# A hybrid attention step on one core: the gates computed in the combined projection instead of between the tiles of the prompt's attention

## The chip, the core and the metric

The kernel runs on one core of one Trainium2 chip. The metric is the device time of one execution in microseconds (us). A core has a matrix engine (TensorE, PE in the profile; PEld is its weight load), VectorE (DVE), ScalarE (ACT), GpSimd (POOL), and SyncE (SP), whose queue here only starts DMAs. Each runs its own instructions in order; semaphores tie them together.

## The reference, cut to what matters

Two layers, each over nine tiles of 128 rows: eight of the prompt (1024 rows) and one of the running streams (8 streams of 16 rows).

```python
h = jnp.einsum('bsd,de->bse', x, w_in)          # 1024 -> 7592 columns
(a_q, a_k, a_v, a_f, a_g, b_q, b_k, b_v, b_g,
 c_ql, c_kvl, c_pe, c_g, gates) = jnp.split(h, IN_OFFSETS, axis=-1)
...                                              # three attentions, 8 heads each
up = jnp.einsum('bsnw,nwd->bsnd', br, w_br)
mixed = (jax.nn.sigmoid(gates.reshape(B, S, 3, D_MODEL)) * up).sum(axis=2)
y = jnp.einsum('bsd,de->bse', mixed, w_o)
```

`gates` are the last 3 x 1024 columns of the combined projection. They are needed only in the up projection, after all attention. Attention a is causal over 1024 keys with forgetting, b sees at most 256 keys and has a sink, c is block-causal over 1024 keys.

## The kernel before

Phases run one after the other, with a barrier between them: per layer the projection, two small phases (forget sums, latent keys), the prompt's attention a, b and c, the streams' attention, the up projection and the output projection. Intermediate results go through scratch tensors in HBM.

**Precision.** A product of fp32 quality is made of three fp32r matmuls: weights and activations are each split into a high and a low part, and high x high, high x low and low x high are summed (L351 to L353, L1056 to L1058). The activations' parts, `xh` and `xl`, stay in SBUF from the projection to the end of attention c.

**Projection** (`projections`, tile names `proj_`). `CHUNKS` lists nine column chunks, all but one 512 wide (the last 424). Each chunk goes over the nine row tiles: 8 x 3 matmuls into one of eight PSUM banks, then ACT or DVE turns the bank into `out`, and SP stores it. While chunk c is multiplied, ACT (L321) and DVE (L326) split the weights of chunk c+1, and SP loads those of c+2. So TensorE has its weights ready one chunk ahead.

**Prompt attention** (`prompt_attention`, names `att_a_`, `att_b_`, `att_c_`). Four passes, each over a pair of heads; a pass has 16 steps, n = 0 to 15, of 128 queries each (the first 8 are one head, the rest the other; a = n mod 8 is the query tile). In a and c a step works on a+1 key tiles, in b on at most 2. The order of each engine's work is one list, `order`, and for each step it has

- `turn` n: TensorE transposes the probabilities (L1027); DVE, and ACT for the first four tiles where there are more than four, copy them to SBUF as `pt` (L1128, L1085);
- `score` n+2: TensorE makes the logits two steps ahead (L1009, mask L1012, in b a sink column L1005); DVE takes the maximum (L1133), ACT the exponential (L1091);
- `fill`, in nine steps of sixteen: one row tile of a gate strip 256 columns wide (below);
- `prep`, in eight steps: a transposition of queries or keys for a later head (L995);
- `pv` n: probabilities times values (L1045), which needs `pt`; then DVE scales and stores to `o` (L1172).

```python
fills = [0, 1, 2, 6, 7, 8, 9, 14, 15]
...
for n in range(K):
    order += [("turn", n), ("score", n + 2)]
    if n in fills:
        order.append(("fill", fills.index(n)))
    if n in preps:
        order.append(("prep", preps[n]))
    order.append(("pv", n))
```

The last pass has no `prep` for a further head and no `score` in steps 14 and 15. A fill is 24 matmuls of 256 columns into one PSUM bank `gacc`, followed by a tanh on ACT into `gout` (L1105; the up projection makes the sigmoid of it). A pass covers one strip for all nine row tiles; four passes make the 1024 gate columns of a branch. A strip's weights come in one DMA (L910) and are split into `gwh` and `gwl`: for the first pass by ACT (L1118) and DVE (L1185), for the others by GpSimd (L968, L970) during the pass before. `gout` is stored in three parts (L916).

SP's queue of a pass: queries and keys of the next pass, gate weights, a gate store, then the store of the first head's output (L902), a wait for its landing, the load of that head's next values (L897) and of its output gates `sg` (L898), two gate stores, and the same for the second head.

Of the kernel before, what the change touches and what calls it, by code (L numbers as in the profile page):

```python
# [21 lines left out]
F32 = mybir.dt.float32  # L22
F32R = mybir.dt.float32r
# [191 lines left out]
def norm_rows(nc, dve, ch, x, gb, st, mv, var_ready, std_ready, t, normed):  # L215
# [16 lines left out]
    ("silu_c", [(O_CG, 512)]),  # L232
    ("cq_bk", [(O_CQ, QR), (O_BK, 128)]),
# [6 lines left out]
def projections(nc, C, T, S, l):  # L240
# [45 lines left out]
    with nc.Block() as block:  # L286
# [95 lines left out]
        def _(act):  # L382
# [20 lines left out]
            for c in range(NCH):  # L403
                kind, u = CHUNKS[c][0], c % 2
                for t in range(NT):
# [9 lines left out]
                    elif kind.startswith("silu"):  # L415
                        nc.scalar.activation(sig[:, j, :], bank, ACT.Sigmoid).then_inc(sig_ready, 1)
                    elif kind in ("cq_bk", "bv_ckv"):
# [101 lines left out]
def _scratch(name):  # L519
    return lambda T, S, l, t: S[name][t * P:(t + 1) * P]  # L520


_HEADS = ("l b s h d -> l (b s) (h d)", "l b s h d -> l (b s) (h d)")
# [8 lines left out]
    "silu_c": [(0, 512, _scratch("sg2"))],  # L532
    "cq_bk": [(0, QR, _scratch("ql")), (QR, 512, _scratch("kb"))],
# [230 lines left out]
def prompt_attention(nc, C, T, S, l, kind):  # L764
# [27 lines left out]
    xh, xl = C["xh"], C["xl"]  # L792
    GW = D // (H // 2)
    graw = ph.sb("graw", [P, KT, GW])
    gwh = ph.sb("gwh", [P, 2 * KT, GW], F32R)
    gwl = ph.sb("gwl", [P, 2 * KT, GW], F32R)
    gout = ph.sb("gout", [P, NT, GW])
    gacc = ph.ps("gacc", [P, 512])
    gw_loaded, gw_hi, gw_lo = ph.sem("gw_loaded"), ph.sem("gw_hi"), ph.sem("gw_lo")
    g_made, g_taken, g_stored = ph.sem("g_made"), ph.sem("g_taken"), ph.ring("g_stored", 3)  # L800
# [25 lines left out]
    fills = [0, 1, 2, 6, 7, 8, 9, 14, 15]  # L826
    preps = {2: (1, 0), 3: (1, 1), 4: (1, 2), 5: (1, 3), 10: (2, 0), 11: (2, 1), 12: (2, 2), 13: (2, 3)}
    assert len(fills) == NT
    order = []
    for n in range(K):  # L830
        order += [("turn", n), ("score", n + 2)]
        if n in fills:
            order.append(("fill", fills.index(n)))
        if n in preps:
            order.append(("prep", preps[n]))
        order.append(("pv", n))
# [41 lines left out]
    with nc.Block() as block:  # L878
        @block.sync
        def _(sp):  # L880
# [25 lines left out]
            wsrc = T["w_in"].rearrange("l (k p) n -> l p k n", p=P)  # L906

            def load_gate(pair):
                col = O_GATE + D * branch + GW * pair
                sp.dma_start(graw[:], wsrc[l, :, :, ds(col, GW)]).then_inc(gw_loaded, 16)  # L910

            def store_gate(pair, part):

                ts = slice(part * NT // 3, (part + 1) * NT // 3)
                sp.wait_ge(g_taken, 1 + NT * pair + ts.stop)
                sp.dma_start(S["gates"].rearrange("(t p) c -> p t c", p=P)  # L916
                             [:, ts, ds(D * branch + GW * pair, GW)], gout[:, ts, :]).then_inc(g_stored[part], 16)


            sp.sem_inc(g_taken, 1)  # L920
            for part in range(3):
                sp.sem_inc(g_stored[part], 16)
            load_qk(0, 0)
            load_gate(0)
# [3 lines left out]
            with sp.Fori(0, H // 2 - 1) as i:  # L928
                sp.wait_ge(tr_made, group(i, 0))
                load_qk(i + 1, 0)  # L930
                sp.wait_ge(gw_lo, i + 1)
                load_gate(i + 1)
                store_gate(i, 0)
# [5 lines left out]
                store_gate(i, 1)  # L939
                store_gate(i, 2)  # L940
# [3 lines left out]
            store_gate(H // 2 - 1, 0)  # L944
            store(H // 2 - 1, 0)
            store_gate(H // 2 - 1, 1)
            store_gate(H // 2 - 1, 2)
# [3 lines left out]
            for part in range(3):  # L951
                sp.wait_ge(g_stored[part], 16 * (H // 2 + 1))

        @block.gpsimd
        def _(pool):

# [7 lines left out]

            def split(pair, at):

                pool.wait_ge(gw_loaded, 16 * (pair + 1))
                nc.gpsimd.tensor_copy(gwh[:, ds(at, KT), :], graw[:]).then_inc(gw_hi, 1)  # L968
                pool.wait_ge(gw_hi, pair + 1)
                nc.gpsimd.tensor_tensor(gwl[:, ds(at, KT), :], graw[:], gwh[:, ds(at, KT), :].bitcast(F32),  # L970
                                        ALU.subtract).then_inc(gw_lo, 1)


            pool.wait_ge(gw_hi, 1)
            split(1, KT)
            with pool.Fori(0, H // 2 - 2) as i:
                pool.wait_ge(g_made, NT * (i + 1))
                split(i + 2, KT * (i & 1))

        @block.tensor  # L980
        def _(pe):
# [33 lines left out]
            def body(i, order, at):  # L1015
                for what, n in order:
# [31 lines left out]
                    elif what == "fill":  # L1048
                        if n == 0:
                            pe.wait_ge(gw_lo, i + 1)  # L1050
                        pe.wait_ge(g_taken, 1 + NT * i + n)
                        first = KT * (i & 1)
                        for kt_ in range(KT):
                            hi, lo = (m[:, kt_, n * P:(n + 1) * P] for m in (xh, xl))
                            wh, wl = (m[:, ds(first + kt_, 1), :].rearrange("p k n -> p (k n)") for m in (gwh, gwl))
                            nc.tensor.matmul(gacc[:, 0:GW], hi, wh, start=kt_ == 0, stop=False)  # L1056
                            nc.tensor.matmul(gacc[:, 0:GW], hi, wl, start=False, stop=False)  # L1057
                            mm = nc.tensor.matmul(gacc[:, 0:GW], lo, wh, start=False, stop=kt_ == KT - 1)  # L1058
                        mm.then_inc(g_made, 1)
# [23 lines left out]
        def _(act):  # L1083
# [10 lines left out]
            def body(i, order, at):  # L1094
                for what, n in order:
# [5 lines left out]
                    if what == "fill":  # L1101
                        if n % 3 == 0:
                            act.wait_ge(g_stored[n // 3], 16 * (i + 1))
# [1015 lines left out]
```

## Time and profile before

| | us |
|---|---|
| median of three runs | 3794.53 |
| their range | 3792.19 to 3799.66 |
| the profiled execution, its own time | 3789.74 |
| its span, first to last instruction | 3788.1 |
| TensorE busy | 3390.3 |
| DVE / ACT / GpSimd busy | 1411.7 / 885.1 / 125.5 |
| mean granted clock of TensorE | 0.952 of 2.4 GHz |

The profile is one execution. Times of rows count from the span's start. A matmul's duration in a row runs to its modelled end and overlaps with the next one, so what a stream of matmuls costs is read from start to start, not from the durations. The two layers run the same program; the first layer's stretches are shown.

### The profile page before, as it was taken

What the parts mean: (1) busy time and instruction counts of PE and PEld (TensorE: products, weight loads), DVE (VectorE), ACT (ScalarE), POOL (GpSimd) and SP (SyncE); (2) the same over time, 40 slices, a digit from 0 to 9 for tenths busy, and PEclk for the clock granted to TensorE, in tenths of its full rate; (3) what the DMA queues carried; (4) which work ended last, traced back from release to release, by engine and by line L of the source; (5) the groups of instructions that cost most, each with busy time, mean ns of one, the idle gap of its engine ahead of it and who ended that gap; (6) DMA issues with size and microseconds to landing.
All of it is one profiled execution on the core that took longest, in us unless ns stands there. A gap on an engine that the chain in (4) does not pass through costs nothing. (4 is left out here: it accounts for less than half of the span.)

```text
span 3788.1 us, 54850 instructions
## 1 busy us (share of the span) xinstructions
PE 3390.3 (89%) x20866; PEld 2834.0 (75%) x20866; DVE 1411.7 (37%) x3261; ACT 885.1 (23%) x1982; POOL 125.5 (3%) x64
## 2 busy tenths in 40 slices
PE   0999978998998997989969999789989999978988
PEld 0888865887997885667758888568879878855877
DVE  5114233333343332354631233334333333323556
ACT  1221212332222332220221112123322233322110
POOL 0000000100100000000000000000000001000000
PEclk9999988999999998989979999889999989988999
DMA  5322225221433225753442222342233243186533
GB/s 194 106 89 94 77 89 160 62 64 39 108 76 98 59 72 142 244 220 126 144 153 92 88 91 67 120 123 64 64 74 91 60 98 87 37 231 212 218 129 107
DMA packets 485460, 423.06 MB, mean 112 GB/s; under 512 B 300452, under 2 KB 394532, under 8 KB 482916
## 3 DMA queue, kind: packets, MB, share of 16 engines
q1 hardware_dynamic: 451444, 381.06, 33.7%
q10 hardware_dynamic: 33840, 39.66, 3.2%
q8 instruction: 110, 1.80, 0.2%
q14 instruction: 66, 0.54, 0.0%
HBM read 295.36 MB, written 127.64 MB: 112 GB/s over the span
## 5 line engine op out<-in xcount | busy, mean ns | idle before, releaser
L351 PE MATMUL proj_acc<-proj_wh,keep_xh 128*128 128x512 f32 (+1 forms) x1296 | 502.1, 387 | 12.5 <-DVE proj_wl L326 12.5
L352 PE MATMUL proj_acc<-proj_wl,keep_xh 128*128 128x512 f32 (+1 forms) x1296 | 500.8, 386 | 0.0
L353 PE MATMUL proj_acc<-proj_wh,keep_xl 128*128 128x512 f32 (+1 forms) x1296 | 500.7, 386 | 0.0
L351 PEld LDWEIGHTS proj_acc<-proj_wh,keep_xh 128*128 128x128 f32 x1296 | 244.5, 189 | 58.4 <-DVE proj_wl L326 13.3
L352 PEld LDWEIGHTS proj_acc<-proj_wl,keep_xh 128*128 128x128 f32 x1296 | 244.6, 189 | 45.7
L353 PEld LDWEIGHTS proj_acc<-proj_wh,keep_xl 128*128 128x128 f32 x1296 | 244.4, 189 | 45.7
L1820 PE MATMUL up_acc<-up_wh,up_bh 128*128 128x512 f32 x432 | 173.1, 401 | 12.8 <-DVE up_wl L1864 12.8
L326 DVE TENSOR_TENSOR proj_wl<-proj_raw,proj_wh 128x512 fp32r<-128x512 f32 (+1 forms) x144 | 96.1, 676 | 210.6 <-ACT proj_wh L321 210.6
L1056 PE MATMUL att_c_gacc<-att_c_gwh,keep_xh 128*128 (+1 forms) x576 | 170.7, 296 | 2.9 <-DVE att_c_gwl L1185 2.9
L1056 PE MATMUL att_b_gacc<-att_b_gwh,keep_xh 128*128 (+1 forms) x576 | 170.7, 296 | 2.3 <-DVE att_b_gwl L1185 2.3
L1056 PE MATMUL att_a_gacc<-att_a_gwh,keep_xh 128*128 (+1 forms) x576 | 169.9, 295 | 1.9 <-DVE att_a_gwl L1185 1.9
L1821 PE MATMUL up_acc<-up_wl,up_bh 128*128 128x512 f32 x432 | 170.4, 394 | 0.0
L1822 PE MATMUL up_acc<-up_wh,up_bl 128*128 128x512 f32 x432 | 170.2, 394 | 0.0
L1057 PE MATMUL att_c_gacc<-att_c_gwl,keep_xh 128*128 (+1 forms) x576 | 164.7, 286 | 0.0
L1057 PE MATMUL att_b_gacc<-att_b_gwl,keep_xh 128*128 (+1 forms) x576 | 164.6, 286 | 0.0
L1058 PE MATMUL att_c_gacc<-att_c_gwh,keep_xl 128*128 (+1 forms) x576 | 164.6, 286 | 0.0
L1058 PE MATMUL att_b_gacc<-att_b_gwh,keep_xl 128*128 (+1 forms) x576 | 164.5, 286 | 0.0
L1057 PE MATMUL att_a_gacc<-att_a_gwl,keep_xh 128*128 (+1 forms) x576 | 163.9, 285 | 0.0
L1058 PE MATMUL att_a_gacc<-att_a_gwh,keep_xl 128*128 (+1 forms) x576 | 163.6, 284 | 0.0
L1091 ACT ACTIVATE att_a_p<-att_a_ss,att_a_stat 128x128 f32<-128x128 f32 (+7 forms) x128 | 95.1, 743 | 255.5 <-DVE att_a_stat L1133 255.4
L1091 ACT ACTIVATE att_c_p<-att_c_ss,att_c_stat 128x128 f32<-128x128 f32 (+7 forms) x128 | 95.1, 743 | 252.9 <-DVE att_c_stat L1133 252.9
L1009 PE MATMUL att_a_ss<-att_a_kt,att_a_qt 66*128 66x512 f32 (+3 forms) x384 | 148.3, 495 | 1.7 <-DVE att_a_kt L1128 1.7
(338 smaller groups left out, 6803.6 us busy)
## 6 DMA issues: line engine op xcount, KB each, us to landing
up_gates<-scratch_gates SPq DMA_DIRECT2D x18, 1536.0 KB, 8.3
proj_raw<-in_w_in SPq DMA_DIRECT2D x48, 512.0 KB, 3.8
str_ka<-in_cache_a_kT SPq DMA_DIRECT2D x16, 1024.0 KB, 9.0
str_va<-in_cache_a_v SPq DMA_DIRECT2D x16, 1024.0 KB, 5.3
scratch_sg<-proj_out SPq DMA_DIRECT2D x54, 256.0 KB, 2.1
up_br<-scratch_br SPq DMA_DIRECT2D x54, 256.0 KB, 8.2
scratch_gates<-att_a_gout SPq DMA_DIRECT2D x24, 384.0 KB, 2.6
scratch_gates<-att_b_gout SPq DMA_DIRECT2D x24, 384.0 KB, 2.7
```

The costliest lines, as they stand in the source:

```text
L326: nc.vector.tensor_tensor(wl[:, u, kt, 0:w], raw[:, kt // 2, kt % 2, 0:w], wh[:, u, kt, 0:w].bitcast(F32), ALU.subtract).then_inc(w_ready[ ...
L351: nc.tensor.matmul(bank, hi, wh[:, u, kt, 0:w], start=kt == 0, stop=False)
L352: nc.tensor.matmul(bank, hi, wl[:, u, kt, 0:w], start=False, stop=False)
L353: mm = nc.tensor.matmul(bank, lo, wh[:, u, kt, 0:w], start=False, stop=kt == KT - 1)
L1009: nc.tensor.matmul(ss[:, s, c:c + cw], lhs, kt[:, u, first + c:first + c + cw], start=True, stop=not last)
L1056: nc.tensor.matmul(gacc[:, 0:GW], hi, wh, start=kt_ == 0, stop=False)
L1057: nc.tensor.matmul(gacc[:, 0:GW], hi, wl, start=False, stop=False)
L1058: mm = nc.tensor.matmul(gacc[:, 0:GW], lo, wh, start=False, stop=kt_ == KT - 1)
L1091: nc.scalar.activation(p[:, s, 0:w], ss[:, s, 0:w], ACT.Exp, bias=stat[:, s, 0:1], accum_out=stat[:, s, 1:2]).then_inc(exp_ready, 1)
L1820: nc.tensor.matmul(acc[:, a, :], bh[:, u, k, :], wh[:, k, cols], start=k == 4 * n, stop=False)
L1821: nc.tensor.matmul(acc[:, a, :], bh[:, u, k, :], wl[:, k, cols], start=False, stop=False)
L1822: mm = nc.tensor.matmul(acc[:, a, :], bl[:, u, k, :], wh[:, k, cols], start=False, stop=k == 4 * n + 3)
```

## The change

The nine fills of each pass, with all that belongs to them (loads, splits, tanh, stores, semaphores), are taken out of `prompt_attention`, and six chunks of 512 columns are added to the projection's list, between `silu_c` and `cq_bk`. The chunks use the projection's path: weights split by ACT and DVE, the tanh on ACT into `out`, one store per row tile.

```diff
@@ CHUNKS
     ("silu_c", [(O_CG, 512)]),
+    *[(f"gate{g}", [(O_GATE + 512 * g, 512)]) for g in range(6)],
     ("cq_bk", [(O_CQ, QR), (O_BK, 128)]),
@@ projections, scalar
+                    elif kind.startswith("gate"):
+                        nc.scalar.activation(out[:, j, :], bank, ACT.Tanh, scale=0.5).then_inc(out_ready[u], 1)
@@ STORES
+    **{f"gate{g}": [(0, 512, _columns("gates", 512 * g, 512))] for g in range(6)},
@@ prompt_attention
-    fills = [0, 1, 2, 6, 7, 8, 9, 14, 15]
...
-        if n in fills:
-            order.append(("fill", fills.index(n)))
@@ sync
-                sp.wait_ge(gw_lo, i + 1)
-                load_gate(i + 1)
-                store_gate(i, 0)
@@ tensor
-                    elif what == "fill":
...
@@ scalar
-            act.wait_ge(gw_loaded, 16)
-            nc.scalar.activation(gwh[:, 0:KT, :], graw[:], ACT.Copy).then_inc(gw_hi, 1)
@@ vector
-            dve.wait_ge(gw_hi, 1)
-            nc.vector.tensor_tensor(gwl[:, 0:KT, :], graw[:], gwh[:, 0:KT, :].bitcast(F32), ALU.subtract)\
-                .then_inc(gw_lo, 1)
```

TensorE in the last pass of attention a, steps 6 to 8, before. `att_a_gacc` is the gate's bank, `att_a_oo` the output of `pv`, `att_a_tr` that of `turn`, `att_a_ss` the logits:

```order
L1058 MATMUL att_a_gacc<-att_a_gwh,keep_xl 128x256
L1045 MATMUL att_a_oo<-att_a_v,att_a_pt 128x64 x7
L1027 MATMUL att_a_tr<-keep_ident,att_a_p 128x128 x8
L1009 MATMUL att_a_ss<-att_a_kt,att_a_qt 128x256
L1012 MATMUL att_a_ss<-keep_mask_a,keep_ident 128x128
L1056 MATMUL att_a_gacc<-att_a_gwh,keep_xh 128x256
L1057 MATMUL att_a_gacc<-att_a_gwl,keep_xh 128x256
```

The same place after:

```order
L978 MATMUL att_a_tr<-keep_ident,att_a_p 128x128 x7
L960 MATMUL att_a_ss<-att_a_kt,att_a_qt 128x128
L963 MATMUL att_a_ss<-keep_mask_a,keep_ident 128x128
L996 MATMUL att_a_oo<-att_a_v,att_a_pt 128x64 x7
L978 MATMUL att_a_tr<-keep_ident,att_a_p 128x128 x8
L960 MATMUL att_a_ss<-att_a_kt,att_a_qt 128x256
L963 MATMUL att_a_ss<-keep_mask_a,keep_ident 128x128
L996 MATMUL att_a_oo<-att_a_v,att_a_pt 128x64 x8
```

The 24 gate matmuls between the mask (L1012, now L963) and `pv` (L1045, now L996) are gone, so `pv` follows the mask directly.

SP at the start of attention b, before:

```order
L892 DMA att_b_q<-scratch_qb 128x8x64
L893 DMA att_b_k<-scratch_kb 128x8x64
L910 ISA
L910 DMA att_b_graw<-in_w_in 128x8x256
L892 DMA att_b_q<-scratch_qb 128x8x64
L893 DMA att_b_k<-scratch_kb 128x8x64
L897 DMA att_b_v<-scratch_vb 128x8x64
L898 DMA att_b_sg<-scratch_sg 128x8x64
```

and after:

```order
L887 DMA att_b_q<-scratch_qb 128x8x64
L888 DMA att_b_k<-scratch_kb 128x8x64
L887 DMA att_b_q<-scratch_qb 128x8x64
L888 DMA att_b_k<-scratch_kb 128x8x64
L892 DMA att_b_v<-scratch_vb 128x8x64
L893 DMA att_b_sg<-scratch_sg 128x8x64
```

The load of a strip's gate weights is gone from between the loads of the two heads.

## Rows read from the trace of the kernel before

**Rows 1.** Stretches of attention a, b, c, first layer: start:end, length, busy per engine

```profile
640.00:943.00 303.00, 285.13 (x2112) 247.42 (x2112) 114.14 (x289) 95.12 (x214) 19.44 (x9) 0.97 0.27 65
943.00:1166.00 223.00, 209.07 (x1672) 197.08 (x1672) 84.06 (x281) 59.36 (x181) 19.35 (x6) 0.97 0.36 88
1166.00:1469.00 303.00, 284.64 (x2112) 248.04 (x2112) 111.66 (x273) 93.82 (x213) 19.28 (x6) 0.97 0.28 72
```

**Rows 2.** One chunk of the projection, same view, by tile `proj_acc`

```profile
299.00:347.96 48.96, 48.96 (x218) 40.54 (x216) 13.02 (x25) 0.60 (x1) 1.00 0.26 82
```

**Rows 3.** Timeline, last pass of b: start us, us, engine, line, operation

```profile
1143.52 0.39 PE L1027 MATMUL att_b_tr<-keep_ident,att_b_p 128*128 128x128 f32 x2
1144.44 0.36 PE L1056 MATMUL att_b_gacc<-att_b_gwh,keep_xh 128*128 128x256 f32 x1
...
1147.79 0.39 PE L1027 MATMUL att_b_tr<-keep_ident,att_b_p 128*128 128x128 f32 x2
...
1149.19 0.39 PE L1027 MATMUL att_b_tr<-keep_ident,att_b_p 128*128 128x128 f32 x2
```

**Rows 4.** Timeline: a fill's first matmul, TensorE, and the copy that `pv` needs

```profile
715.65 0.36 PE L1056 MATMUL att_a_gacc<-att_a_gwh,keep_xh 128*128 x1
...
715.60 0.56 DVE L1128 COPY att_a_pt<-att_a_tr 128x384 f32<-128x384 f32 x1 [0.48 <-PE att_a_tr L1027]
...
721.43 0.37 PE L1056 MATMUL att_a_gacc<-att_a_gwh,keep_xh 128*128 x1
...
721.17 0.69 DVE L1128 COPY att_a_pt<-att_a_tr 128x512 f32<-128x512 f32 x1 [0.59 <-PE att_a_tr L1027]
...
726.92 0.36 PE L1056 MATMUL att_a_gacc<-att_a_gwh,keep_xh 128*128 x1
...
727.32 0.29 DVE L1128 COPY att_a_pt<-att_a_tr 128x128 f32<-128x128 f32 x1
...
1009.98 0.36 PE L1056 MATMUL att_b_gacc<-att_b_gwh,keep_xh 128*128 x1
...
1010.14 0.29 DVE L1128 COPY att_b_pt<-att_b_tr 128x128 f32<-128x128 f32 x1
...
1254.59 0.36 PE L1056 MATMUL att_c_gacc<-att_c_gwh,keep_xh 128*128 x1
...
1254.42 0.29 DVE L1128 COPY att_c_pt<-att_c_tr 128x128 f32<-128x128 f32 x1
```

**Rows 5.** Timeline, last pass of b, step 14, which has no score

```profile
1153.53 0.36 PE L1056 MATMUL att_b_gacc<-att_b_gwh,keep_xh 128*128 128x256 f32 x1
...
1153.81 0.42 DVE L1128 COPY att_b_pt<-att_b_tr 128x256 f32<-128x256 f32 x1
```

**Rows 6.** Timeline: TensorE restarting after a copy by DVE, at two places

```profile
648.19 0.69 DVE L1128 COPY att_a_kt<-att_a_tr 66x512 f32<-66x512 f32 x1 [0.17 <-PE att_a_tr L995]
...
649.02 0.55 PE L1009 MATMUL att_a_ss<-att_a_kt,att_a_qt 66*128 66x128 f32 x1 [0.87 <-DVE att_a_kt L1128]
...
1027.33 0.69 DVE L1128 COPY att_b_kt<-att_b_tr 65x512 f32<-65x512 f32 x1
...
1028.27 0.24 PE L1005 MATMUL att_b_ss<-att_b_kt,att_b_qt 65*128 65x1 f32 x1 [0.35 <-DVE att_b_kt L1128]
```

**Rows 7.** Attention a's start: timeline, and the first fill's stretch (TensorE alone, granted clock)

```profile
651.34 2.28 DVE L1185 TENSOR_TENSOR att_a_gwl<-att_a_graw,att_a_gwh 128x2048 fp32r<-128x2048 f32 x1
...
652.41 0.31 PE L1012 MATMUL att_a_ss<-keep_mask_a,keep_ident 128*128 128x128 bf16 x1
...
653.95:658.30 4.35, 4.33 (x24) 0.64 1.21 288
```

**Rows 8.** SP's timeline in b, and DMA issues in b (times, KB, us to landing)

```profile
985.48 0.40 SPq L902 DMA_DIRECT2D scratch_br<-att_b_o  x1
988.08 0.37 SPq L897 DMA_DIRECT2D att_b_v<-scratch_vb  x1
...
att_b_sg<-scratch_sg SPq DMA_DIRECT2D x8, 256.0 KB, 3.8
```

More of the change, by code:

```diff
@@ L520, in _scratch, with _columns @@
     return lambda T, S, l, t: S[name][t * P:(t + 1) * P]
+def _columns(name, at, width):
+    return lambda T, S, l, t: S[name][t * P:(t + 1) * P, at:at + width]
 _HEADS = ("l b s h d -> l (b s) (h d)", "l b s h d -> l (b s) (h d)")
@@ L791, in prompt_attention @@
     oo = ph.ps("oo", [P, 512])
[L792 to L800, printed above, removed]
     const_ready, chain = ph.sem("const_ready"), ph.sem("chain")
@@ L825, in prompt_attention @@
     K = 2 * PT
-    fills = [0, 1, 2, 6, 7, 8, 9, 14, 15]
     preps = {2: (1, 0), 3: (1, 1), 4: (1, 2), 5: (1, 3), 10: (2, 0), 11: (2, 1), 12: (2, 2), 13: (2, 3)}
-    assert len(fills) == NT
     order = []
@@ L905, in _ @@
                 sp.dma_start(sinks[HD:HD + 1, :], T["sinks"][ds(l, 1), :]).then_inc(sinks_loaded, 16)
[L906 to L922, printed above, removed]
             load_qk(0, 0)
-            load_gate(0)
             load_qk(0, 1)
@@ L938, in _ @@
                 load_v(i + 1, 0)
-                store_gate(i, 1)
-                store_gate(i, 2)
                 store(i, 1)
@@ L943, in _ @@
                 load_v(i + 1, 1)
-            store_gate(H // 2 - 1, 0)
             store(H // 2 - 1, 0)
-            store_gate(H // 2 - 1, 1)
-            store_gate(H // 2 - 1, 2)
             store(H // 2 - 1, 1)
@@ L950, in _ @@
                 sp.wait_ge(o_stored[u], 16 * (H // 2))
-            for part in range(3):
-                sp.wait_ge(g_stored[part], 16 * (H // 2 + 1))
         @block.gpsimd
@@ L963, in _ @@
                 nc.gpsimd.memset(kt[0:HD, :, SEQ:SEQ + 1], 0.0).then_inc(const_ready, 1)
[L965 to L978, printed above, removed]
         @block.tensor
@@ L1047, in body @@
                         mm.then_inc(pv_made, 1)
-                    elif what == "fill":
[L1049 to L1059, printed above, removed]
             if kind != "c":
@@ L1100, in body @@
                     s = n % 2
-                    if what == "fill":
-                        if n % 3 == 0:
-                            act.wait_ge(g_stored[n // 3], 16 * (i + 1))
-                        act.wait_ge(g_made, NT * i + n + 1)
-                        nc.scalar.activation(gout[:, n, :], gacc[:, 0:GW], ACT.Tanh, scale=0.5).then_inc(g_taken, 1)
-                    elif what == "turn" and len(at[what, n]) == 2:
+                    if what == "turn" and len(at[what, n]) == 2:
                         g = at[what, n][0]
```

## The prediction

> **What bounds the kernel now.** I read the stretches by stage first. In all three attentions TensorE is busy for some 94% of the time, DVE for 37% and ACT for 27 to 31% [rows 1]; the rest is mostly at the ends of the phases, where nobody has work. In the projection TensorE is busy for all of a chunk's 48.96 us [rows 2]. So TensorE's queue sets the time in both places, and an edit is worth what it does to the starts of its matmuls. In attention a part of that is cover: a fill stands between `score` and `pv`, and while it runs DVE and ACT catch up. I therefore price three things: the matmuls added, the matmuls taken out, and the waits that the fills cover. All sums are for one layer and are doubled at the end; the two layers are alike.
>
> **Added: six chunks.** Each has the same 216 matmuls of 512 columns as the chunk shown, 48.96 us from start to start at full clock [rows 2], that is 226.7 ns for one. ACT and DVE have room: in the chunk shown DVE works for 13 us on banks of the projection, and a gate chunk asks only for nine tanhs and the usual splitting of weights. 6 x 48.96 = **+293.8 us**, all on the path. Nothing of it is hidden, since no engine but TensorE is full there.
>
> **Taken out: 108 fills** (3 attentions x 4 passes x 9). In the last pass of b a step with a fill and no prep runs from 1143.52 to 1147.79, 4.27 us; the next, with neither, from 1147.79 to 1149.19, 1.40 us [rows 3]. Both are free of waits and otherwise the same, so a fill is worth 2.87 us, 119.6 ns for one of its 24 matmuls. 108 x 2.87 = **-310.0 us**. The work is the same in both forms, yet two 256-column matmuls take 239 ns and one of 512 columns 227 ns: that is the gain of the wider form, 16.2 us a layer. The difference comes from the width alone; whichever part of it is weight load I need not know.
>
> The Trainium skill, page "TensorE: Matmul & The Clock Gate", section "Back-to-back issue gap", gives the isolated spacing as N/2.4 + 2.5 ns. By that, 256 and 512 columns would take 109.2 and 215.8 ns, the 108 fills 283.0 us and the six chunks 279.7, and only 3.3 us a layer would be gained instead of 16.2. The rows disagree with it for this stream of alternating weight loads, and the sum goes by the rows.
>
> **New waits.** Without the fill, TensorE reaches `pv` 0.03 us after the moment at which it now starts the fill (one mask's spacing), but it must wait until DVE's copy `pt` has ended, and restart. The restart after a DVE copy took 649.02 - (648.19 + 0.69) = 0.14 us with one wait and 1028.27 - (1027.33 + 0.69) = 0.25 us with several and registers between them [rows 6]; `pv` has one last wait, so I take 0.14 and keep 0.25 for the range. Wait = copy's end + 0.14 - (fill's start + 0.03) [rows 4]:
> - a, step 6 (or 14): 715.60 + 0.56 + 0.14 - 715.68 = 0.62
> - a, step 7 (or 15): 721.17 + 0.69 + 0.14 - 721.46 = 0.54
> - a, step 0 of a pass: 727.32 + 0.29 + 0.14 - 726.95 = 0.80. In front of this copy DVE has two small operations for the next head and the loop's branch. For step 8, which has the two operations but not the branch, I estimate 0.34.
> - b, step 0: 1010.14 + 0.29 + 0.14 - 1010.01 = 0.56
> - c, step 0: 1254.42 + 0.29 + 0.14 - 1254.62 = 0.23, in step 8 nothing.
>
> Steps 1, 2 and 9 have one or two tiles to copy and a long `score` ahead of `pv`; I expect none there. The same holds for b's other steps: the step of 1.40 us shows DVE and ACT keeping up without a fill or a prep [rows 3]. In the last pass steps 14 and 15 lose their `score` as cover as well. In b that is 1153.81 + 0.42 + 0.14 - 1153.56 = 0.81 each [rows 5]; in a and c it adds some 0.71 together.
> - a: 8 x (0.62 + 0.54) + 3 x 0.80 + 4 x 0.34 + 0.7 = 13.7
> - c: the same shapes, 8 x 1.16 + 3 x 0.23 + 0.7 = 10.7
> - b: 3 x 0.56 + 2 x 0.81, and 0.3 for small ones = 3.6
>
> Sum **+28.0 us**. The softmax chain itself (maximum, exponential, two steps ahead) I hold for hidden: in b's bare step it fits into two steps of 1.40 us.
>
> **The starts of the three phases.** Before, the first fill waits for DVE's split `gwl` of 2.28 us and then runs at a granted clock of 0.64, in 4.35 us, so `pv` of step 0 starts at 658.30 [rows 7]. After, it can start soon after the mask at 652.41, some 5.7 us earlier; 2.87 of that is in the sum already. Against the other 2.8: TensorE was at the low clock then, and steps 1 to 3 will run at it in place of the fill, for up to 2 us of loss. I take 0.8 us gain a phase, **-2.5 us**, between +3 us a phase (clock up as early, most of its low time spent waiting) and -2 us (clock up later).
>
> GpSimd's splits and the gate DMAs go too; nobody on the path waits for them after the start of a phase.
>
> **The sum.** 293.8 - 310.0 + 28.0 - 2.5 = +9.3 us a layer, +18.6 for two. The profiled execution, 3789.74 us (span 3788.1), would become 3808.3. It lies 4.8 us below the median of the runs shown, 3794.53; from the median the forecast is 3813 us, 0.5% slower. A measurement of this kernel can tell about 0.2%, 7.6 us, from no change.
>
> **Rivals.**
> - *The wider matmuls win* (the other side). The order looks two steps ahead, and if the short waits are absorbed, by copies that start earlier once ACT and DVE have no gate work, what is left is -16.2 - 2.5 = -18.7 a layer, 3757 us. It decides at the waits: above 18.7 us a layer the change loses, below it wins. For it: busy shares of DVE and ACT are low. Against: before the copies in question DVE had been idle for 0.48 and 0.59 us, waiting for TensorE's transposes [rows 4]; they cannot start earlier. Chance 0.10.
> - *Half of the waits.* If they come to between 15 and 22 us a layer, the time is within 7.6 us of the old one: 3794 in the middle, against my 28.0. Chance 0.12.
> - *The values of b come late.* SP stores a head's output, waits for the landing, and only then loads that head's next values. Store to next issue is 988.08 - 985.48 = 2.60 us, then some 0.9 us of issues and 3.8 us to land [rows 8]: 7.3 us. Before, eight steps of b took 223 / 8 = 28 us [rows 1]; now 8 x 1.40 and, as an estimate, 2 more for four preps, 13. It still fits. If landings double under the denser traffic, `pv` or the scaling after it waits some 2 us, 7 times a layer: +14 us a layer at the worst, 3840; as a case I put it at 3832. Chance 0.09.
> - *The clock falls.* At the start of each phase the granted clock is 0.64 while TensorE had been waiting [rows 7]; the mean over the phases is 0.97 [rows 1]. With holes of 0.5 to 0.8 us in the short steps it may fall to 1.2 GHz. The attention's 829 us a layer [rows 1] become 547, 1094 for two; if the work of a tenth of that runs at that level, it costs some 100 us: 3910. The Trainium skill, same page, section "A second HAM failure mode: psum-queue depth-cycling", reports just this, a matrix engine with short pauses between groups swinging between the two levels. Against it in this trace: b's bare step kept its spacing of 1.40 us [rows 3]. Chance 0.05.
>
> **How the numbers follow.** The forecast's case has 0.64, as most of its terms are read start to start in the same trace. Slower by over 0.2%: 0.64 + 0.09 + 0.05 = 0.78; within: 0.12; faster: 0.10. Range: a restart of 0.25 us instead of 0.14 on 47 waits a layer adds 10 us, starts that lose 2 us a phase add 6 x 2.8 = 17, and a few late values 8: 3848. Downwards, starts that gain 3 us a phase give 6 x 2.2 = 13, and waits of 22 us a layer another 12: 3788. Left out are the first rival and the last, 0.15.
>
> **What would show it.** After: chunks of the projection still 48.96 us apart, fifteen of them; a pass of a shorter by some 22.4 us (9 x 2.87 less, 3.4 more), one of b by some 25.2; `pv` (L996) with idle time in front of it, ended by DVE's copy of `pt`, about 28 us a layer; no idle of TensorE behind the exponential. I would be wrong where steps 1, 2 or 9 wait as well, where `pv` restarts more slowly than 0.14 us, or where the granted clock dips inside a phase.

## The result

The changed kernel takes 4038.74 us (median of four executions, 3995.97 to 4061.48), against 3795.16 for the kernel before beside it. The ratio of the means is 1.0603 [1.0516, 1.0691], taken without the slowest execution, which was over 1.5% above the fastest: slower by 6%, where 0.5% was forecast, and outside the forecast's range. The profiled execution took 4029.46 us, 239.7 more than the profiled one before; the forecast had +18.6.

| phase | before, layer 1 / 2 | after, layer 1 / 2 | difference | forecast a layer |
|---|---|---|---|---|
| projection | 463.1 / 464.6 | 757.6 / 757.3 | +294.5 / +292.7 | +293.8 |
| attention a | 293.0 / 293.0 | 240.7 / 216.4 | -52.3 / -76.6 | -90.4 |
| attention b | 213.1 / 213.2 | 193.1 / 191.5 | -20.0 / -21.7 | -100.5 |
| attention c | 293.2 / 293.9 | 202.8 / 201.1 | -90.4 / -92.8 | -93.4 |
| streams' attention | 137.6 / 135.8 | 147.7 / 135.3 | +10.1 / -0.5 | 0 |

Each time runs from the phase's first matmul to its last. The last column sums the prediction's terms by phase: 36 fills x 2.87 less, the waits of that phase more, 0.8 us for the start. Projection and attention c came as forecast. Of the 221 us by which the forecast missed, 159 lie in attention b, 52 in a, 4 in c and 10 in the streams' attention; all the rest together is 4 us the other way.

Where the time went stands in the views by stage. These are stretches of the kernel after: start:end, length, busy time of PE, PEld, DVE, ACT and POOL with the number of instructions, then the granted clock, the share of the DMA engines and GB/s. The first three are a, b and c of layer 1, the next three those of layer 2, the last is the first gate chunk of the projection. They answer to [rows 1, 2]; [rows 2] counts only what touches `proj_acc`.

```profile
939.00:1182.00 243.00, 227.14 (x1248) 174.31 (x1248) 110.75 (x286) 79.56 (x177) 0.00 (x0) 0.79 0.19 40
1182.00:1385.00 203.00, 191.63 (x808) 167.96 (x808) 87.21 (x280) 43.30 (x144) 0.18 (x3) 0.50 0.26 53
1385.00:1598.00 213.00, 188.19 (x1248) 146.06 (x1248) 107.66 (x272) 77.61 (x176) 0.00 (x0) 0.94 0.26 59
2941.00:3160.00 219.00, 200.89 (x1248) 155.05 (x1248) 110.27 (x288) 79.23 (x177) 0.00 (x0) 0.90 0.22 44
3160.00:3361.00 201.00, 189.87 (x808) 166.39 (x808) 87.19 (x280) 43.30 (x144) 0.19 (x3) 0.51 0.27 53
3361.00:3572.00 211.00, 185.88 (x1248) 144.50 (x1248) 107.75 (x272) 77.61 (x176) 0.00 (x0) 0.95 0.28 61
478.96:527.92 48.96, 48.96 (x217) 40.54 (x216) 5.54 (x8) 9.53 (x17) 0.00 (x0) 1.00 0.28 91
```

The matmuls of b fell from 1672 to 808, yet TensorE was busy for 191.63 us instead of 209.07. The column to read is the one behind the busy times: the granted clock of b is 0.50, that is 1.2 GHz, where [rows 1] had 0.97. The gate chunk takes 48.96 us, to the digit of the chunk in [rows 2]; DVE and ACT work for 5.54 and 9.53 us of it and are not in the way.

The page of the profile shows it too, in its line of the granted clock over 40 slices of 100.7 us:

```profile
PE   1999999978989898889869999999789898978988
PEclk9999999986885599879989999999879757989999
```

The two digits 5 stand for attention b of layer 1, the digits 757 for layer 2 (slices that b does not fill). The line above them has 8 and 9 at the same places: TensorE was as busy as ever.

Whole passes, same columns: the second pass of a in layer 1 and in layer 2, the third of a in layer 1, the second of b, the second of c.

```profile
1018.30:1084.20 65.90, 62.93 (x314) 48.26 (x313) 27.88 (x73) 19.68 (x44) 0.00 (x0) 0.72 0.19 40
...
3012.70:3062.40 49.70, 45.24 (x314) 35.25 (x313) 27.39 (x73) 19.35 (x44) 0.00 (x0) 1.00 0.26 53
1084.20:1133.70 49.50, 45.35 (x314) 35.35 (x313) 27.46 (x74) 19.34 (x44) 0.00 (x0) 1.00 0.25 53
...
1244.30:1291.90 47.60, 47.60 (x203) 42.02 (x204) 21.86 (x71) 10.75 (x37) 0.00 (x0) 0.50 0.27 55
1452.80:1501.40 48.60, 45.09 (x314) 35.28 (x313) 26.85 (x68) 19.35 (x44) 0.00 (x0) 1.00 0.29 65
```

The same 314 matmuls of a take 65.9 us in one layer and 49.7 in the other, with nothing different but the clock. b's pass has no idle time at all, 47.60 of 47.60 us, and runs at half the clock. So there are two things to explain: b is always slow, a and c only at their starts (a in layer 1 also in its second pass), and not by the same amount each time.

The step of b that [rows 3] showed at 1.40 us, in the timeline after (start us, us, what, count):

```profile
1217.32 0.63 PE L978 MATMUL att_b_tr<-keep_ident,att_b_p 128*128 128x128 f32 x2
1217.75 0.43 PE L956 MATMUL att_b_ss<-att_b_kt,att_b_qt 65*128 65x1 f32 x2
1218.04 1.20 PE L960 MATMUL att_b_ss<-att_b_kt,att_b_qt 65*128 65x256 f32 x2
1219.03 0.42 PE L963 MATMUL att_b_ss<-keep_mask_b,keep_ident 128*128 128x256 bf16 x1
1219.24 0.95 PE L996 MATMUL att_b_oo<-att_b_v,att_b_pt 128*128 128x64 f32 x4
1219.99 0.42 PE L978 MATMUL att_b_tr<-keep_ident,att_b_p 128*128 128x128 f32 x1
```

From transposition to transposition 2.67 us, without a gap. Half of 2.67 is 1.34, near the 1.40 of before.

### The profile page after: what moved, and what is told of

Read it like the earlier page. It is cut to its first block and busy times, and to the rows that moved or that the text cites. A ratio compares the mean times of both kernels' runs of the same rounds, so it can differ in the third digit from the quotient of the medians.

```text
span 4027.8 us, 49020 instructions
## 1 busy us (share of the span) xinstructions
PE 3610.9 (90%) x18274; PEld 2896.1 (72%) x18274; DVE 1469.7 (36%) x3351; ACT 903.5 (22%) x1964; POOL 9.7 (0%) x28
## 5 line engine op out<-in xcount | busy, mean ns | idle before, releaser
L352 PE MATMUL proj_acc<-proj_wh,keep_xh 128*128 128x512 f32 (+1 forms) x2160 | 838.0, 388 | 12.4 <-DVE proj_wl L327 12.4
L353 PE MATMUL proj_acc<-proj_wl,keep_xh 128*128 128x512 f32 (+1 forms) x2160 | 836.7, 387 | 0.0
L354 PE MATMUL proj_acc<-proj_wh,keep_xl 128*128 128x512 f32 (+1 forms) x2160 | 836.6, 387 | 0.0
L352 PEld LDWEIGHTS proj_acc<-proj_wh,keep_xh 128*128 128x128 f32 x2160 | 406.6, 188 | 92.1 <-DVE proj_wl L327 13.1
L354 PEld LDWEIGHTS proj_acc<-proj_wh,keep_xl 128*128 128x128 f32 x2160 | 406.5, 188 | 79.4
L353 PEld LDWEIGHTS proj_acc<-proj_wl,keep_xh 128*128 128x128 f32 x2160 | 406.7, 188 | 79.0
L996 PEld LDWEIGHTS att_a_oo<-att_a_v,att_a_pt 128*128 128x128 f32 x1152 | 159.1, 215 | 42.2 <-ACT att_a_pt L1024 20.1
L1749 PE MATMUL up_acc<-up_wh,up_bh 128*128 128x512 f32 x432 | 173.2, 401 | 12.8 <-DVE up_wl L1793 12.8
L996 PE MATMUL att_a_oo<-att_a_v,att_a_pt 128*128 128x64 f32 x1152 | 167.9, 297 | 18.0 <-DVE att_a_pt L1060 15.2
L996 PEld LDWEIGHTS att_c_oo<-att_c_v,att_c_pt 128*128 128x128 f32 x1152 | 140.5, 194 | 37.0 <-ACT att_c_pt L1024 24.1
L996 PE MATMUL att_c_oo<-att_c_v,att_c_pt 128*128 128x64 f32 x1152 | 149.5, 276 | 16.3 <-DVE att_c_pt L1060 14.1
L960 PE MATMUL att_c_ss<-att_c_kt,att_c_qt 96*128 96x512 f32 (+3 forms) x384 | 150.7, 502 | 1.7 <-DVE att_c_kt L1060 1.7
L996 PEld LDWEIGHTS att_b_oo<-att_b_v,att_b_pt 128*128 128x128 f32 x480 | 118.0, 334 | 19.4 <-issue 14.9
```

The source lines that it names most:

```text
L352: nc.tensor.matmul(bank, hi, wh[:, u, kt, 0:w], start=kt == 0, stop=False)
L353: nc.tensor.matmul(bank, hi, wl[:, u, kt, 0:w], start=False, stop=False)
L354: mm = nc.tensor.matmul(bank, lo, wh[:, u, kt, 0:w], start=False, stop=kt == KT - 1)
L960: nc.tensor.matmul(ss[:, s, c:c + cw], lhs, kt[:, u, first + c:first + c + cw], start=True, stop=not last)
L996: mm = nc.tensor.matmul(oo[:, 0:HD], pt[:, s, j * P:(j + 1) * P], v[:, u, t, :], start=j == 0, stop=j == len(tiles(a)) - 1)
L1749: nc.tensor.matmul(acc[:, a, :], bh[:, u, k, :], wh[:, k, cols], start=k == 4 * n, stop=False)
```

## The experiments

All are edits of the changed kernel unless it is said otherwise. The added matmuls multiply parts of `xh` and `xl` into a PSUM bank `gacc` that nobody reads, so they load TensorE and nothing else. Three theories were set against each other: that the clock follows **which matmuls TensorE streams** (M), that it falls with **holes** in the stream (H), and that it only depends on the **start** of a phase, after the wait for the first loads (S).

### Wide and narrow matmuls in b's old fill steps

`e_wide_b` puts 24 matmuls of 256 columns back into the steps of b that held a fill, `e_narrow_b` 12 fp32 matmuls of 64 columns into the same steps.

```diff
+        if kind in "b" and n in [0, 1, 2, 6, 7, 8, 9, 14, 15]:
+            order.append(("dummy", n))
...
+                    elif what == "dummy":
+                        for kt_ in range(KT):
+                            for m in (xh, xh, xl):
+                                nc.tensor.matmul(gacc[:, 0:256], m[:, kt_, a * P:(a + 1) * P], xl[:, kt_, 0:256],
+                                                 start=True, stop=True)
```

The narrow one has, in the same place:

```diff
+                        for kt_ in range(12):
+                            m = (xh, xl)[kt_ % 2]
+                            nc.tensor.matmul(gacc[:, 0:HD], m[:, kt_ % KT, a * P:(a + 1) * P].bitcast(F32),
+                                             xl[:, kt_ % KT, 0:HD].bitcast(F32), start=True, stop=True)
```

> The changed kernel, with a stand-in for the fills in attention b alone: in the nine steps 24 matmuls of 256 columns on the activations' parts, with no weights to load or split, no tanh, no store (the results are not used; the output is the reference's). It adds some 103 us of matmuls a layer to b at full clock. Theory M (the granted clock follows the mix of matmuls: b's own are short or narrow, and never raise it): b is granted the full clock soon after its start, as before the change, and takes about 213 us instead of 192, so about 20 us a layer more for 103 us of added work, 4070 in all. Theory H (short waits keep the clock down): the same, since the waits are covered too. Theory S (the clock stays down because a phase starts with it down): also the same, if the first fill raises it.

> As e_wide_b, but each stand-in is 12 fp32 matmuls of 64 columns, the form of pv, about as long (some 2.7 us at full clock) and covering the same waits, with little streamed. Theory M: the clock stays at 1.2 GHz through b; the stand-ins then cost twice as much, b takes about 380 us, 4400 in all. Theory H: the waits are covered, the clock goes up, b takes some 205 us, 4055 in all. Theory S: undecided, since the start is as narrow as the rest.

The wide one took 4056.61 us, the narrow one 4411.07, beside 3801.01 for the kernel before. Attention b of layer 1, from its first matmul to its last, in the wide one:

```profile
1165.00:1375.50 210.50, 207.31 (x1672) 195.95 (x1672) 81.37 (x278) 43.75 (x144) 0.00 (x0) 0.98 0.23 46
```

and in the narrow one:

```profile
1187.70:1562.90 375.20, 374.33 (x1671) 351.64 (x1672) 87.20 (x278) 43.75 (x144) 0.00 (x0) 0.50 0.13 26
```

Both have 1672 matmuls, the extra ones in the same steps, and no idle time to speak of. With the wide ones the clock is 0.98 and the second pass takes 51.61 us, against 51.62 with real fills. With the narrow ones, TensorE is busy for 374.33 of 375.20 us and gets 0.50 throughout, in both layers. H falls: a stream without holes does not hold the clock. All three theories had expected the result of the wide one, so it only confirms that b can be lifted; the narrow one separates them. Width and type (fp32r against fp32) were changed together here, and which of them counts is not told apart.

### Raising the clock ahead of b

`e_warm_b` puts 30 matmuls of 512 columns ahead of b's first transposition, while it waits for its loads.

```diff
+            if kind in "b":
+                for w in range(30):
+                    nc.tensor.matmul(gacc[:], xh[:, w % KT, 0:P], xl[:, w % KT, 0:512], start=True, stop=True)
```

> The changed kernel with 30 matmuls of 512 columns ahead of the first transposition of attention b, while its first loads are under way; results not used. Theory S: the clock is up when the steps begin and stays up, b's four passes take some 105 us instead of 186, 3880 in all. Theory M: the clock goes up and falls again within b, whose time stays near 190, 4035 in all. Theory H: as M.

4030.49 us, and b took 199.6 and 199.3 us, most of it at the low clock. Four stretches of its first layer, cut where the clock changes; the 30 wide matmuls run from 1159.1 to 1168.6, b's own work follows:

```profile
1157.40:1164.20 6.80, 5.07 (x12) 4.04 (x13) 0.14 (x1) 0.00 (x0) 0.18 (x3) 0.50 0.61 129
1164.20:1174.40 10.20, 8.88 (x51) 6.86 (x50) 2.51 (x7) 2.10 (x6) 0.00 (x0) 1.00 1.00 178
1174.40:1184.00 9.60, 9.60 (x43) 8.48 (x41) 4.13 (x14) 2.46 (x9) 0.00 (x0) 0.50 0.01 2
1184.00:1358.00 174.00, 172.97 (x734) 152.07 (x733) 80.08 (x258) 38.63 (x131) 0.00 (x0) 0.50 0.21 44
```

The clock rises, b begins at 2.4 GHz, and 6 us after the last wide matmul it falls again. In these 6 us TensorE waits twice, 0.25 and 0.94 us, for the first copies of `qt` and `kt`; from 1171.8 on, across the fall, it has no idle time, and in the 174.00 us that follow only 1.03. S falls for b: a start at the high clock does not last. What b streams did not keep it up, nor bring it back.

### Doses of wide matmuls

`e_one_b` puts one matmul of 512 columns into each of b's 16 steps, `e_half_b` one into every second step, `e_quarter_b` one into every fourth; `e_two_b` puts two into each. `e_half_b` and `e_quarter_b` also have 20 such matmuls ahead of attention a. The edit of `e_one_b`:

```diff
+        if kind in "b" and n in range(K):
+            order.append(("dummy", n))
...
+                    elif what == "dummy":
+                        nc.tensor.matmul(gacc[:], xh[:, a, a * P:(a + 1) * P], xl[:, a, 0:512], start=True, stop=True)
```

> The changed kernel with one extra matmul of 512 columns in each of the 16 steps of a pass of attention b (3.6 us a pass at full clock, against 25.8 for the nine fills); its result is not used. Theory M: if so small a dose is enough, b goes from 192 to about 121 us, 3890 in all; if not, it stays at 1.2 GHz and costs 7 us a pass more, 4085. Theory H: no wait is covered, the clock stays down, 4085. Theory S: stays down, 4085.

> The changed kernel with two additions whose results are not used: 20 matmuls of 512 columns at the start of attention a, and one in every second step of b (8 a pass, 1.8 us at full clock). Theory M, if half the dose still holds the clock up: a 205 to 210 us, b about 125, 3855 in all, which is what the sum of the prediction comes to when the clock is out of it, with some 40 us for the additions and slow starts. If half the dose is too little: b near 195, 4000. Theory S says of a that its first pass is fast in both layers.

> As e_half_b with one extra matmul in every fourth step of b (4 a pass, 0.9 us). Theory M says the clock in b depends on how much is streamed, so somewhere below one matmul a step it must fail: b either about 122 us (3850 in all) or 195 (4000).

| kernel | wide matmuls a pass | median (executions) | b, layer 1 / 2 | b's clock |
|---|---|---|---|---|
| changed kernel | 0 | 4038.74 (4) | 193.1 / 191.5 | 0.50 / 0.51 |
| `e_quarter_b` | 4 | 3951.05 (1) | 143.3 / 187.7 | 0.75 / 0.54 |
| `e_half_b` | 8 | 3879.27 (4) | 134.8 / 132.8 | 0.83 / 0.84 |
| `e_one_b` | 16 | 3903.47 (1) | 131.6 / 133.1 | 0.91 / 0.89 |
| `e_one_b_2` (the same again) | 16 | 3927.49 (4) | 131.7 / 133.1 | 0.91 / 0.89 |
| `e_two_b` | 32 | 3930.49 (4) | 142.3 / 142.5 | 0.94 / 0.93 |

One pass of b in `e_one_b`:

```profile
1198.50:1228.40 29.90, 29.11 (x219) 25.24 (x219) 20.38 (x70) 10.78 (x38) 0.00 (x0) 1.00 0.43 88
```

One pass of b in `e_half_b`:

```profile
1200.20:1228.40 28.20, 27.41 (x211) 24.03 (x212) 20.38 (x70) 10.72 (x37) 0.00 (x0) 1.00 0.45 93
```

For `e_one_b` H and S had both expected a clock that stays down and 4085 us; it took 3903.47. With eight wide matmuls a pass the kernel takes 3879.27 us, ratio 1.0243 [1.0213, 1.0274]. There is more work in a pass than in the changed kernel, and it takes 28.2 us instead of 47.6. The eight extra matmuls cost 8 x 0.227 = 1.8 us at the chunk's spacing, so b's own work at full clock takes 28.2 - 1.8 = 26.4 us a pass (worked out, since b never ran at full clock without wide matmuls). That is 25.2 less than the 51.6 of before, the prediction's figure. `e_one_b` gives nearly the same, 29.9 - 3.6 = 26.3. The forecast's arithmetic for b was right for a clock that b did not get.

`e_quarter_b` shows both levels. A pass of b in its first layer and one in its second:

```profile
1256.40:1283.70 27.30, 26.55 (x208) 23.36 (x208) 20.39 (x71) 10.77 (x37) 0.00 (x0) 1.00 0.47 96
3147.10:3196.50 49.40, 49.40 (x208) 43.24 (x208) 21.98 (x71) 10.79 (x37) 0.00 (x0) 0.50 0.26 53
```

The same 208 matmuls in the same order, once at each level, in one execution. In the second layer the clock rose only in the last pass.

The 20 wide matmuls ahead of a in these two kernels answer the question of S for a. The first two passes of a in the second layer of `e_half_b`:

```profile
2825.90:2885.80 59.90, 54.81 (x355) 42.63 (x356) 29.55 (x77) 22.73 (x51) 0.13 (x2) 0.97 0.36 67
2885.80:2951.80 66.00, 62.95 (x314) 48.35 (x313) 27.97 (x72) 19.68 (x44) 0.00 (x0) 0.72 0.19 40
```

In all four layers of the two kernels the first pass took 59.7 to 59.9 us, as S says. But in three of the four the clock fell again in the short steps of the second pass, which then took 66.0 us instead of 49.7. A raised start carried a through its first pass and not through the phase.

Does one matmul a step always hold b's clock? The kernel was run again beside one with two.

> The kernel of e_one_b once more, timed: one extra matmul of 512 columns a step in b and nothing at any phase's start. e_hold has shown executions 86 and 183 us above its best, as if b's clock had stayed down in one layer or in both. If the cause is that e_hold's matmuls at the start leave b's first steps elsewhere in the chip's measure of activity, this kernel without them stays within 3880 to 3935 (the first pass of a accounts for the rest). If one matmul a step is simply close to the limit, some executions here are again 85 or 170 us longer.

> The changed kernel with two extra matmuls of 512 columns in each step of b (7.3 us a pass), nothing else. Theory M: b is at full clock in every execution, 106 + 29 us and a slow start, about 145 a layer; 3930 in all with the 40 us of spread that a's first passes bring, and none 85 us longer. It stays slower than the kernel before: the doses that hold the clock cost what they save.

`e_one_b` again: 3907.52, 3925.00, 3929.99 and one execution of 4059.48. `e_two_b`: 3904.83 to 3946.14, none apart. Against the kernel before, 1.0326 [1.0281, 1.0371] without the one apart, and 1.0337 [1.0282, 1.0391]. So an execution can lose some 130 us with one wide matmul in every step, of the size of b staying low through most of both layers; its mean granted clock was 0.893, against 0.923 to 0.933 in the others. It was not profiled, and that b was the cause is argued, not shown. With two a step none of the four executions stood apart; in the profiled one b held the high clock after its first pass, at a price of 10 us a layer (142.4 against 131.7 and 133.1), and the kernel is still 3.4% slower than before.

### The gates of b left where they were

`e_bgates` leaves b's fills in attention b and moves only the gates of a and c, four chunks.

```diff
+    *[(f"gate{g}", [(O_GATE + 512 * g, 512)]) for g in [0, 1, 4, 5]],
...
+    GATE = kind in "b"
...
-        if n in fills:
+        if GATE and n in fills:
```

> One part of the change alone: the gates of branches a and c are computed in the projection (four chunks), those of branch b stay as fills in its attention. Theory M: b is at full clock as in the kernel before (213 us a layer); per layer +195.8 for four chunks, -91 in c, and in a between -88 (clock up from the first pass) and -52 (clock down through the first pass): 3830 to 3900 in all, near 3855. That is some 180 us less than the whole change, which would place the loss in b's gates. If the loss came from the projection's longer list or from a and c, this kernel would stay above 3950.

3841.13 us (3829.39 to 3848.20), ratio 1.0122 [1.0102, 1.0142]. A pass of b (second, layer 1), then the first and the second pass of a:

```profile
1129.10:1180.80 51.70, 51.00 (x419) 48.41 (x419) 20.58 (x71) 14.34 (x45) 6.46 (x2) 1.00 0.38 94
841.30:912.50 71.20, 67.94 (x337) 51.70 (x338) 29.91 (x76) 23.17 (x51) 0.00 (x0) 0.71 0.24 44
912.50:961.90 49.40, 45.31 (x314) 35.31 (x313) 27.42 (x73) 19.35 (x44) 0.00 (x0) 1.00 0.25 53
```

Four fifths of the loss are gone (50 us over the kernel before instead of 244): b took 213.2 and 214.4 us, as before. The terms of the prediction for a and c alone give 12 us a layer, 24 in all. Its profiled execution was 57.5 above the median of before. The rest is attention a, 215.8 and 223.7 against 202.6 each by the prediction's terms, 34 us more, all of it in first passes at a low clock such as the 71.2 us above. The first pass of a in `e_one_b`, whose a is the changed kernel's, took 59.7 us:

```profile
938.70:998.40 59.70, 54.90 (x337) 41.95 (x338) 29.75 (x76) 22.84 (x51) 0.00 (x0) 0.89 0.29 52
```

Same 337 matmuls, 11.5 us apart. In the profiled layers where a runs without wide matmuls and without warming, it took 204.9 us once, 215.8 to 223.7 in five of them, and 240.6 or 240.7 in the others. In all of them the clock comes up within the first pass, early or late. In the slowest it then falls in the short steps at the start of the second pass (1020.0 to 1057.6 us in the changed kernel, with 37.34 of 37.55 us busy), and rises again.

### Warming a phase's start in the kernel before, and holding the clock all through

`f_before_warm` is the kernel before with 14 matmuls of 512 columns ahead of the first transposition of a, b and c. `e_hold` is the changed kernel with the same, one in every step of b, and two in each of the steps 0, 1, 2, 8, 9 and 10 of a and c.

```diff
+            if kind in "abc":
+                for w in range(14):
+                    nc.tensor.matmul(gacc[:], xh[:, w % KT, 0:P], xl[:, w % KT, 0:512], start=True, stop=True)
```

> The kernel before the change, fills and all, with 14 matmuls of 512 columns at the start of each of the three attentions, while their first loads are under way; the results are overwritten. Each phase there begins with the granted clock at half, and the first fill took 4.35 us instead of 2.9. Theory M: the clock is up when the first steps begin, and since the fills follow at once it stays up; 3 to 4 us less in each of the six phases, 3791 - 20 = 3771, faster by 0.5%. Theory S says the same. Against it: the additions reach beyond the wait for the loads and cost 1 to 2 us a phase; then no change.

> The changed kernel with matmuls whose results are not used wherever the clock was seen to fall: 14 of 512 columns at the start of each attention, one in each step of b, two in steps 0, 1, 2, 8, 9 and 10 of a and c; 73 us of added matmuls in two layers. Theory M: the clock holds from the start of each attention to its end, in all executions, a takes some 212 us in both layers, b 128, c 210; 3880 in all with a spread of under 15 us (the changed kernel alone spread over 65). If the low first pass of a had another cause than its short steps, it would still show, at 66 instead of some 52 us.

`f_before_warm` (12 executions): 3790.11 beside 3791.97, ratio 0.9988 [0.9977, 0.9998], where 20 us less were expected. The start of attention a, cut where the clock changes:

```profile
638.80:642.40 3.60, 3.60 (x9) 2.83 (x10) 0.00 (x0) 0.00 (x0) 0.12 (x2) 0.50 0.67 142
642.40:649.30 6.90, 4.70 (x29) 3.17 (x27) 2.74 (x7) 3.39 (x4) 0.00 (x0) 0.99 1.20 273
649.30:656.10 6.80, 5.31 (x21) 4.53 (x22) 3.02 (x6) 2.47 (x7) 0.00 (x0) 0.50 1.22 227
656.10:725.30 69.20, 67.53 (x512) 58.94 (x511) 26.79 (x67) 22.26 (x51) 6.45 (x2) 1.00 0.17 46
```

The wide matmuls end at 643.9. The clock is up from 642.4 and falls at 649.3, while TensorE waits 2.45 us for ACT's first exponential, and it comes up again only in the first fill, at 656.1 (657.1 without the warming). The first `pv` starts at 656.98 instead of 658.30, so 1.3 us are won there and not 3 to 4. This fall follows both narrow work and a wait, and the run does not tell them apart.

`e_hold` was profiled near the expected total, 3874.05 us, with a at 218.3 and 218.7 (expected 212), b at 126.4 and 132.8, c at 212.9 and 212.7. In a the clock was not held from the start: it fell for 10.2 us after the warming, and the first pass took 66.1 and 66.4 us at a mean of 0.89, where some 52 were expected; the second passes then kept 1.00. b's second pass:

```profile
1197.60:1227.50 29.90, 29.10 (x219) 25.25 (x219) 20.39 (x70) 10.76 (x37) 0.00 (x0) 1.00 0.44 88
```

The other three executions took 3891.90, 3977.81 and 4057.46 us, at mean clocks of 0.949, 0.926 and 0.906 against 0.957. A spread under 15 us was expected; it was 183. The steps of 86 and 166 us above 3891.90 are near what b lost in the changed kernel by staying low, 80 us a layer. That it was b in these two is argued from the sizes alone. With `e_one_b_2` it says that one wide matmul a step did not hold the clock every time.

## Why the prediction was wrong

**What held.** The chunks: six for +294.5 and +292.7 us, forecast 293.8, at 48.96 us each. A fill's worth at full clock: a pass of a became 49.4 from 71.6, 22.2 shorter (forecast 22.4), one of c 23.0 shorter, one of b 25.2 by way of `e_half_b` (forecast 25.2). Next to no idle time behind the exponential (0.4 us once, in a of layer 2). The waits, in the view that lists what TensorE waited for (us in all, times, longest), for c in layer 1:

```profile
PE att_c_oo L996 <- DVE att_c_pt L1060: 6.9, 16, 0.9
PE att_c_tr L978 <- ACT att_c_qt L1024: 6.0, 7, 1.0
PE att_c_oo L996 <- ACT att_c_pt L1024: 1.1, 1, 1.1
```

and for a in layer 2:

```profile
PE att_a_oo L996 <- DVE att_a_pt L1060: 7.9, 16, 1.0
PE att_a_tr L978 <- ACT att_a_qt L1024: 5.1, 6, 1.0
PE att_a_oo L996 <- ACT att_a_pt L1024: 1.1, 1, 1.1
PE att_a_ss L960 <- DVE att_a_kt L1060: 0.9, 1, 0.9
PE att_a_tr L978 <- ACT att_a_p L1030: 0.4, 1, 0.4
```

`pv` waits for DVE's copy 16 times, 6.9 and 7.9 us, with one wait for ACT's copy 8.0 and 9.0; forecast 10.7 and 13.7. The waits of `turn` for ACT's `qt` were there before. The two can't be set side by side as they are: the view counts from the modelled end of the matmul before, the forecast from start to start. From start to start, in a of the changed kernel without and with a wait (step 6):

```profile
1086.79 0.22 PE L963 MATMUL att_a_ss<-keep_mask_a,keep_ident 128*128 128x128 bf16 x1
1086.85 0.27 PE L996 MATMUL att_a_oo<-att_a_v,att_a_pt 128*128 128x64 f32 x1
...
1102.77 0.22 PE L963 MATMUL att_a_ss<-keep_mask_a,keep_ident 128*128 128x128 bf16 x1
1103.46 0.29 PE L996 MATMUL att_a_oo<-att_a_v,att_a_pt 128*128 128x64 f32 x1 [0.46 <-DVE att_a_pt L1060]
```

0.69 - 0.06 = 0.63 us, forecast 0.62, where the view has 0.46. Counted so, all waits of `pv` come to some 11.0 us in c of layer 1 (forecast 10.7) and 12.8 in a of layer 2 (13.7, part of it covered by the low clock of the first pass). Places, kind and size of the waits were right there. For b the view has only this:

```profile
PE att_b_oo L996 <- DVE att_b_pt L1060: 1.0, 2, 0.5
PE att_b_ss L956 <- issue: 0.8, 1, 0.8
```

At half the clock TensorE hardly waits for anybody. That is why the wait views, where I would have looked for a loss, show less of it than forecast while b runs 21 us a pass over its forecast.

**The step that failed** is the last rival, "the clock falls", and with it the term "taken out", which took each fill's 2.87 us as saved on a stream that keeps 2.4 GHz. Three things in that rival were wrong.

- *Its size and chance.* It gave a tenth of the attention at the low clock, 100 us, with a chance of 0.05. What fell was all of b, 47.6 - 26.4 = 21.2 us a pass and a little less in the first and the last, which makes the 159 us that b missed by.
- *Its cause.* It looked for the loss in "holes of 0.5 to 0.8 us in the short steps". `e_narrow_b` had 374.33 of 375.20 us busy and got 0.50; the passes of a and c with waits of up to 1.1 us kept 1.00. By the holes b, with the fewest of them, was the safest phase, and it was the one that fell.
- *The evidence against it.* "B's bare step kept its spacing of 1.40 us [rows 3]" is true and proves little. That step stands among fills, nine steps of sixteen. In `e_warm_b` the high clock outlived the last wide matmul by 6 us, which is four such steps. A clock that follows what was streamed can't be read from one step of 1.40 us. Where b's own work stood alone in that trace, ahead of its first fill, the clock did fall, at 954.0:

```profile
954.00:960.90 6.90, 6.35 (x27) 5.57 (x28) 3.09 (x5) 0.91 (x4) 0.00 (x0) 0.51 1.10 236
```

It rose again only at 960.9, late in the fill that began at 956.4. Two waits, 0.82 and 0.66 us, came just ahead of the fall, so this was a warning and not a proof.

What the forecast said beside the clock came close. Of the 239.7 us between the profiled executions, the misses in b and a are 159 and 52, nearly all of it made by the clock; what is left, as an estimate, is 29 us, 10 of them in the streams' attention, against the +18.6 of the sum. The sum's other terms came close together, and it put at nothing the one that counted.

The Trainium skill, page "TensorE: Matmul & The Clock Gate", section "HAM oscillation — how this bites in real kernels", puts the rule as having no gaps of an idle TensorE, and its advice is a loop without waits for DMAs. The rule is silent on this case: the granted clock was 0.50 in `e_warm_b` over 174.00 us with 172.97 busy. The section on psum-queue depth-cycling, which the prediction cited, speaks of pauses between groups too, and b's middle passes had none. What the runs show is one thing beside it: matmuls kept TensorE busy and did not raise its clock.

**The other terms.** The starts: forecast -2.5 us a layer, from "clock up as early" to 2 us lost a phase. Phase c came at 201 to 203 us, so its start was about right. For a the bound was far too small: its first pass lost 20 us in layer 1 and 12 in layer 2 against what its terms give (82.1 us before, less 22.4, is 59.7; it took 79.3 and 71.2), and the second pass another 16.5 in layer 1. The fills had brought the clock up at step 0 [rows 7]; I read their 4.35 us at 0.64 as a cost, and it was the price of the rest of the phase. The values of b were not late: their landing took 3.1 us (values) and 3.7 (output gates), as before, and TensorE never waited for them. The gain from wider matmuls, 16.2 us a layer, was real and small.

The 10 us of the streams' attention in layer 1, which holds nothing of the change, came with a granted clock of 0.85 where it was 0.90 before; in other kernels it took 135 to 148 us in either layer. It was not studied.

**No version beat the kernel before.** b's own work ran whole passes at 2.4 GHz only with wide matmuls beside it, and every kernel in which it did so through both layers, with all six chunks moved, was 2 to 3% slower (`e_wide_b`, with the full 24 a fill, 7%). The gate matmuls were such a filler, and they did work that had to be done anyway: 36 of them a layer took 103 us in b, the two chunks that replace them take 98, and without them the rest of b takes 193 us instead of 110.

**What stays open.** What decides the level from one execution or layer to the next, where the same code shows both. Whether it is the width of a matmul or its type that counts; `e_narrow_b` changed them together. Two other candidates are weakened by the traces. The share of time with a weight load running was 93% in `e_wide_b` at 0.98 (195.95 of 210.50 us) and 94% in `e_narrow_b` at 0.50. Transpositions were 63 of 203 matmuls in b's pass at 0.50, and 104 of 314 in a pass of a at 1.00. What a and c have and b lacks are logits of up to 512 columns in one matmul (b at most 256); that this keeps their clock up was not tested, nor why c came up in its first pass each time and a often late. Fills of 512 columns inside attention were not tried: a strip twice as wide, with its two parts, asks for twice the SBUF there.

## What to carry to other kernels

Before you move wide matmuls out of a phase, ask what TensorE streams when they are gone, and look for a stretch of the same trace in which that mix runs alone for a pass or more; a single step between wide matmuls still ran at their clock here. Busy time and wait views don't show a low clock, since a slow engine is busy and waits for nobody: read the granted clock of each stretch beside them. Work that seems to fill a phase's gaps may also be what holds the clock for everything around it, and then its removal costs more than it took.

## What was new about the hardware

- A stream that keeps TensorE busy almost without a gap can stay at 1.2 GHz: 374.33 of 375.20 us busy at a granted 0.50 with fp32 matmuls of 64 columns, and 0.98 with fp32r matmuls of 256 columns in the same steps.
- A few wide matmuls can lift everything around them: four of 512 columns in a pass of b could do so (27.3 us at 1.00) or fail to (49.4 us at 0.50); eight did in every profiled pass after the first.
- The same code takes different times: attention a, with the same instructions, from 205 to 241 us, and the executions of `e_hold` lie 183 us apart where those of the kernel before beside it lay within 15.
- fp32r matmuls of 256 columns with alternating weights cost 119.6 ns each, those of 512 columns 226.7 ns: the wider form gains 5%.
